# Two key selections interleaved with the attention units: the second block's third and fourth query groups

## What is computed

```python
def dsa_branch(q, k, v, q_idx, k_idx, w_idx, topk):      # topk = 128
    def one_block(i):                                    # 128 queries, one query group
        s = einsum('bqhd,bkd->bqhk', qib, k_idx32)       # 8 index heads
        score = einsum('bqhk,bqh->bqk', relu(s), wb)
        score = where(causal, score, -inf)
        _, sel = lax.top_k(score, topk)                  # 128 keys for each query
        ...                                              # attention over the selected keys
    return lax.map(one_block, arange(4))

def swa_branch(q, k, v, sinks):    # window of 128 keys, 8 heads, a sink logit for each head
    ...

o_a, o_b = dsa_branch(...), swa_branch(...)
mix = sigmoid(g_a) * (o_a @ w_branch_a) + sigmoid(g_b) * (o_b @ w_branch_b)
x = x + mix @ w_out
...
```

## Time and profile before

| | us |
|---|---|
| median of 3 runs | 2515.87 |
| lowest and highest run | 2512.0 and 2522.29 |
| the profiled execution | 2523.43 |
| its span, first to last instruction | 2521.6 |
| TensorE busy in it | 2402.2 |
| VectorE busy | 1358.4 |
| GpSimd busy | 1118.5 |
| ScalarE busy | 963.1 |
| mean granted TensorE clock, 1 is full | 0.960 |

### The profile page before, as it was taken

The page is one execution under the profiler, slowest core; times in us unless marked ns, Lnnn a source line. Parts: engine busy times, 40 slices in busy tenths (PEclk is TensorE's granted clock), DMA queues, the critical chain, the costliest instruction groups (busy, mean ns, idle before and its releaser), DMA issues.

```text
span 2521.6 us, 29250 instructions
## 1 busy us (share of the span) xinstructions
PE 2402.2 (95%) x10742; PEld 1903.6 (75%) x10742; DVE 1358.4 (54%) x2070; ACT 963.1 (38%) x1525; POOL 1118.5 (44%) x553
## 2 busy tenths in 40 slices
PE   4989799999999999889999999999999999999998
PEld 4876577878888878757787888887775678788886
DVE  6799844974523799983557122257567442411222
ACT  3347442332331434765233233235533433322332
POOL 2578512533444548872263444462431014444443
PEclk7999889989999999999998999999999899999999
DMA  6522101625545523221122233332221012223332
GB/s 237 188 88 69 58 26 40 214 92 186 166 131 183 167 69 99 69 76 34 34 84 70 89 106 93 100 92 71 85 84 34 1 34 92 83 92 100 96 96 75
DMA packets 215206, 239.88 MB, mean 95 GB/s; under 512 B 9722, under 2 KB 188730, under 8 KB 215098
## 3 DMA queue, kind: packets, MB, share of 16 engines
q1 hardware_dynamic: 215098, 238.45, 29.6%
HBM read 236.32 MB, written 2.10 MB: 95 GB/s over the span
## 4 chain that ended last, share of the span: by engine, by line
PE 80%; DVE 10%; issue 2%; ACT 1%; POOL 1%; DMA 0%; DVEq 0%; SPq 0%; ACTq 0%; POOLq 0%
PE product L2250 22%; PE product L2252 22%; PE product L2251 22%; DVE side L1673 5%; PE side L2760 2%; PE product L2326 2%; PE side L2553 2%; PE product L2577 1%; PE side L2770 1%; PE product L2782 1%; PE side L2319 1%; PE side L2312 1%; PE side L2571 1%; DVE slot_r L1778 1%; PE side L2346 1%
## 5 line engine op out<-in xcount | busy, mean ns | idle before, releaser
L873 POOL TENSOR_TENSOR ring_low<-ring_f,ring_high 128x1024 fp32r<-128x1024 f32 (+1 forms) x349 | 846.5, 2431 | 1248.9 <-ACT ring_high L982 1247.9
L2250 PE MATMUL product<-slot_r,ring_high 128*128 128x512 f32 x2792 | 1107.7, 397 | 38.0 <-DVE slot_f L1763 9.0
L2252 PE MATMUL product<-slot_r,ring_high 128*128 128x512 f32 x2792 | 1094.8, 392 | 0.0
L2251 PE MATMUL product<-slot_r,ring_low 128*128 128x512 f32 x2792 | 1094.6, 392 | 0.0
L2250 PEld LDWEIGHTS product<-slot_r,ring_high 128*128 128x128 f32 x2792 | 529.1, 189 | 166.2 <-issue 30.0
L982 ACT ACTIVATE ring_high<-ring_f 128x1024 fp32r<-128x1024 f32 (+1 forms) x349 | 367.6, 1057 | 705.6 <-DMA ring_f<-in_w_ff 340.0
L2252 PEld LDWEIGHTS product<-slot_r,ring_high 128*128 128x128 f32 x2792 | 528.6, 189 | 112.9
L2251 PEld LDWEIGHTS product<-slot_r,ring_low 128*128 128x128 f32 x2792 | 529.7, 190 | 111.1 <-issue 1.7
L1639 DVE SCALAR_TENSOR_TENSOR va<-product,sqt 128x512 f32<-128x512 f32 x96 | 66.3, 692 | 357.1 <-ACT sqt L1062 355.4
L1673 DVE SCALAR_TENSOR_TENSOR side<-slot_f,cols,side 128x512 f32<-128x512 f32 x332 | 220.7, 746 | 0.0
L1652 DVE TENSOR_TENSOR slot_f<-product,slot_f 128x512 f32<-128x512 f32 x64 | 44.2, 690 | 184.2 <-PE product L2252 184.2
(11 more groups left out here) (282 smaller groups left out, 2198.7 us busy)
## 6 DMA issues: line engine op xcount, KB each, us to landing
ring_f<-in_w_ff SPq DMA_DIRECT2D x128, 512.0 KB, 3.6
slot_f<-in_w_ada SPq DMA_DIRECT2D x48, 1024.0 KB, 6.0
ring_f<-in_w_in SPq DMA_DIRECT2D x96, 512.0 KB, 3.7
ring_f<-in_w_out SPq DMA_DIRECT2D x40, 512.0 KB, 3.4
ring_f<-in_w_up SPq DMA_DIRECT2D x32, 512.0 KB, 3.7
ring_f<-in_w_down SPq DMA_DIRECT2D x32, 512.0 KB, 3.4
slot_f<-in_x SPq DMA_DIRECT2D x4, 512.0 KB, 9.1
ring_f<-in_w_v SPq DMA_DIRECT2D x4, 512.0 KB, 3.8
```

Of the source, the lines that this page charges most:

```text
L873: pool.tensor_tensor(whole(ring_low[:, s, :, :], n), whole(ring_f[:, s, :, :], n), whole(ring_high[:, s, :, :], n).bitcast(F32), ALU.subtr ...
L2250: pe.matmul(out_ap, high, rhs_high, start=start, stop=False)
L2251: pe.matmul(out_ap, low, rhs_high, start=False, stop=False)
L2252: return pe.matmul(out_ap, high, rhs_low, start=False, stop=stop)
```

## The change

The scores of qb 2 get a tile of their own: `ada_acc`, 512 columns that only the first block uses. qb 1 and 3 keep the old one. So the third group's scores stay where they are while the fourth group's are added up, and its 16 rounds move out of the score loop. They now stand behind the masked logits of units 0 to 15, and the fourth group's rounds move from there to units 16 to 31.

```diff
-        score = tile(SC, 5)
+        score = [None, tile(SC, 5), ada_acc[:], tile(SC, 5)]
...
             def select(qb, k):
-                sc = score[:, 0:(qb + 1) * P]
+                sc = score[qb][:, 0:(qb + 1) * P]
...
-                own = score[:, n - P:n]
+                own = score[qb][:, n - P:n]
                 steps.did(dve.tensor_tensor(own, own, mask_own, ALU.add))
-                if qb < BLK - 1:
+                if qb == 1:
                     for k in range(ROUNDS):
                         select(qb, k)
...
-                    if u < ROUNDS:
-                        select(BLK - 1, u)
+                    if u < 2 * ROUNDS:
+                        select(2 + u // ROUNDS, u % ROUNDS)
```

More of the change, by code:

```diff
@@ L2111, in _ @@
                 n = (qb + 1) * P
-                sc = score[:, 0:n]
+                sc = score[qb][:, 0:n]
                 wcol = index_w[:, qb * IH + h:qb * IH + h + 1]
```

## The result

| | before | after |
|---|---|---|
| median of 11 runs, us | 2516.33 | 2524.61 |
| lowest and highest | 2508.64, 2522.29 | 2518.77, 2531.03 |
| the profiled execution, its span | 2523.43, 2521.6 | 2521.63, 2519.8 |

The changed kernel takes 1.0032 of the time before, 95% interval 1.002 to 1.0043: 8.3 us by the medians (the interval is 5 to 11 us), slower, and within the 0.5% that the forecast called no measurable change. A second set of runs gave 1.0042 (1.0027 to 1.0057), 11.5 us. The forecast was 10.6 us.

The account below looks back on a forecast made before the run. TensorE was taken as the bound (80% of the chain), with VectorE becoming it in words 2 and 3. 0 + 0 + 7.0 + 3.6 = +10.6 us, shifted to the median: 2526.5 us, range 2519 to 2534 us.

Parts of the forecast that it names:

- Part 1: Score stage: removing the third group's 16 rounds (20.0 us) is worth 0, since they lie beside TensorE's products.
- Part 2: Attention words 0 and 1: lighter rounds shed 4.2 us of VectorE, worth 0 because TensorE is the bound; bounds 0 and -1.
- Part 3: Attention words 2 and 3: added rounds on 512 keys make VectorE the bound, +7.0 us; bounds +6 and +9.
- Part 4: Attention words 2 and 3: TensorE's waits for VectorE let the granted clock fall once for 13.60 us, +3.6 us.
- rival 1: Words 2 and 3: the clock holds, so +7.0 us, 2522.9 us; chance 0.25.
- rival 2: Clock stays low for most of words 2 and 3, falling again after each return: +15.8 us, 2531.7 us; chance 0.20.
- Rival 3: Words 0 and 1 or the score stage: lighter parts give back up to 4.2 us, clock holds: +2.8, 2518.7 us; chance 0.07.

Follow-up runs that it names:

- second profile: The changed kernel run again with no edit, profiled in another execution: +11.5 us against the kernel before (1.0042).
- steadied base: The kernel before with a filler in every second unit of word 4, later set: -4.4 us against the kernel before (0.9978).
- steadied pair: Changed kernel, fillers in every second of units 16 to 39: +1.5 us; kernel before, fillers in every second unit of word 4: -4.4 us.
- spread kernel: Kernel before, fourth group's rounds in every second of units 0 to 31, word 1 fillers every fourth unit: -2.6 us (0.9992).

## Why the prediction was right

**Part 1 (0, measured 0).** The rows of TensorE over the selection decided it: 11.20 of 11.20 us busy. The same window after the change, the 93.7 us of the stage in both kernels, and the kernel relieved of 15 rounds say the same. That ScalarE waited 9.3 us was true and cost nothing.

**Part 2 (forecast 0, bounds 0 to -1; measured -0.3 and +0.4).** Units 0 to 15 went from 32.72 to 32.39 us in the profiled execution after, while VectorE shed 3.9 us of work. The second profile of the changed kernel has 33.12 us there, so the 0.3 us are no gain; what differs between executions is word 0 with its fall of the clock (granted 0.79 and 0.76).

**Part 3 (+7.0, measured +6 to +7.9).** Word 2 came to 17.57 us where the sum had 17.39. Both words with a nearly full clock take 35.6 us (changed kernel, second profile), +7.6; against its own steadied base the whole of it is 5.9 us by medians and 7.2 in the traces. The rule "read the unit's period where that mix already runs" gave the price to a few per cent, since word 1 had the same two loads. What the sum left out is the give-back at the end: the bound of +6 named it, and word 4 shows it at 0.9 us. There is some luck in the closeness: the two words came out 0.6 us above the sum and the give-back 0.9 below it, and the two errors nearly cancel.

**Part 4 (+3.6, right in kind, its place too narrow, its size in part luck).** The sum let TensorE stand still for 0.5 us in every one of the 16 units; the traces list four waits in word 2, of 0.17 to 0.44 us, and in the second profile five in word 3, of up to 0.6 us. The clock fell all the same, at 1960 in the one and 1968.5 in the other, in both 10 to 11 us behind the first wait of word 2; so the forecast of a fall held on a premise that put TensorE's listed waiting about three times too high (4 us a word against 1.2). In the profile after, the clock was low for 17.1 us of word 3 and the excess over 35.6 us was 39.4 - 35.6 = 3.8 us. A unit without filler took 2.5 us at the lower level, from one start of TensorE's logits to the next in word 3 of the changed kernel, where the estimate was 2.4:

```profile
1964.88 1.22 PE L2760 MATMUL side<-slot_f 64*128 64x256 f32 x2
1967.39 1.22 PE L2760 MATMUL side<-slot_f 64*128 64x256 f32 x2
1969.91 1.22 PE L2760 MATMUL side<-slot_f 64*128 64x256 f32 x2
```

The step assumed that a fall inside words 2 and 3 comes on top of the one in word 4, which stays as it was. In the profile after, that is what happened: words 4 and 5 had their fall too, and were 0.9 us shorter than before. In the second profile words 2 and 3 had only 3 us of it, and the fall in words 4 and 5 was 33.5 us long and cost 7.2 us there, which no term had. Over the attention the two executions lie 10.2 and 15.2 us above the kernel before, against medians of +8.3 and +11.5. The forecast of +10.6 lies between the medians, but its clock term is one value for very unequal executions: what the medians leave over the 5.9 us of the steadied pair is 2.4 and 5.6 us.

**The rivals.** The clock did not hold (rival 1), and it was not low through most of words 2 and 3 (rival 2: it was for 17 of 39 us in one profile and for 3 of 36 in the other). The part of rival 2 that says that the clock goes down and up again where TensorE has short waits is what happened: in the profile after it fell at 1960, rose at 1977 and fell again at 1987. "TensorE: Matmul & The Clock Gate" in the Trainium skill, section "A second HAM failure mode: psum-queue depth-cycling", tells of the like in another kernel, with short idle gaps between groups of matmuls. These traces agree in that: waits of 0.3 to 0.4 us ahead of the fall at 1960, and a clock at 0.61 in that word. With a filler in every unit TensorE is busy for 37.17 of 37.17 us in words 2 and 3, and the clock is full there. That the waits are the cause, and which of them brings a fall, is not shown beyond this. Rival 3 would have paid back up to 4.2 us; the runs with only the fourth group's rounds show no difference.

**What stays open.** Which share of the 8.3 to 11.5 us is clock cannot be said to the microsecond, since its falls differ from execution to execution; the steadied pair puts it at 2 to 6 us by the medians, whose own intervals are some 3 us wide to either side. Why the clock stayed low for 33.5 us in words 4 and 5 in one execution of the changed kernel and for some 13.5 us in the other is open, too.

## What to carry to other kernels

A wait is worth what stands behind it: ScalarE's 9.3 us behind a selection were free, since TensorE's products ran over them, while work that went to the "idle half" of VectorE became the bound at once, because a round on 512 keys adds 1.3 us of VectorE's time to a unit (17.15 us busy in word 2 in place of 6.86) where TensorE's own content is 1.66 us and VectorE had 0.86 us of other work already. Before moving work into a loop, add up one period of each engine there and compare them; another stretch of the same loop that already runs the mix gives the number. And look for a stretch in which the clock falls: two filler products in word 4, 1.7 us together, made the kernel before 4.3 us faster, where the change had nothing to give.

## What was not expected of the hardware

The lower clock does not keep its place. Two executions of one kernel had it low for 17 us of word 3 (granted clock 0.61 there) and, in the other, in word 3 hardly at all (0.91) but through words 4 and 5 (0.51 and 0.55), where it cost 7 us more. Between these two executions the attention differs by 5 us of the 11 us that the whole differs by. The rest lies elsewhere, and the kernel before spreads as widely over its runs (2508.6 to 2522.3 us).

Nor does a busy TensorE bring the clock back at once. In the second profile of the changed kernel it was low for 33.5 us in which TensorE was never idle (the window below, most of words 4 and 5):

```profile
1986.00:2019.50 33.50, 33.50 (x97) 21.51 (x97) 8.64 (x40) 9.46 (x36) 0.00 (x0) 0.50 0.00 1
```

Adding matmuls shortened the kernel in each case where they fell into such a stretch: four fillers of 0.86 us in words 2 and 3 by 5.2 us, twelve by 4 to 7.5 us (+4.0 with them, +8.3 and +11.5 without, in different sets of runs), two in word 4 of the kernel before by 4.3 and 4.4 us. In the spread kernel the two gave less, 1.8 us by the medians of two sets (-4.4 against -2.6), and that is within the scatter.
